# Encoder block on one core: the second MLP product as seven block products instead of eight, with weight sums made in DRAM

## What is computed

```
u = _rms(h, norm_mlp)
h = h + square(relu(u @ w_mlp_in)) @ w_mlp_out      # w_mlp_in 1024 x 4096, w_mlp_out 4096 x 1024
return _rms(h, norm_final)[:, N_META:]
```

## Time and profile before

| | |
|---|---|
| Median of three runs | 1323.64 us (1323.58 to 1324.17) |
| Profiled execution, its own time | 1323.88 us |
| Its span, first to last instruction | 1322.1 us |
| TensorE clock granted, mean over the span | 0.993 of full |
| Busy share of the span: PE, DVE, ACT, POOL | 97%, 49%, 35%, 32% |
| Matmuls of the second MLP product | 1152 |
| DMA over the span | 96.17 MB, mean 73 GB/s |

### The profile page before, as it was taken

The page is one execution under the profiler, slowest core; times in us unless marked ns, Lnnn a source line. Parts: engine busy times, 40 slices in busy tenths (PEclk is TensorE's granted clock), DMA queues, the critical chain, the costliest instruction groups (busy, mean ns, idle before and its releaser), DMA issues.

```text
span 1322.1 us, 18548 instructions
## 1 busy us (share of the span) xinstructions
PE 1283.5 (97%) x7181; PEld 1111.3 (84%) x7181; DVE 651.1 (49%) x743; ACT 461.1 (35%) x681; POOL 428.7 (32%) x244
## 2 busy tenths in 40 slices
PE   5999999999999999989999999999999999999996
PEld 4888888888889898878888888888888888888885
DVE  4116999999977777783732131111111233343334
ACT  5234211222266675643521341222222322233335
POOL 1453222233342333327322222222222222222234
PEclk8999999999999999999999999999999999999998
DMA  5222222333211011033352212222222121111112
GB/s 181 73 64 65 64 63 64 100 108 108 87 45 29 20 33 43 21 91 105 102 202 91 64 48 63 61 60 62 60 63 62 64 79 64 64 64 64 64 48 96
DMA packets 123907, 96.17 MB, mean 73 GB/s; under 512 B 9695, under 2 KB 106013, under 8 KB 123852
## 3 DMA queue, kind: packets, MB, share of 16 engines
q1 hardware_dynamic: 121548, 89.12, 22.5%
q10 hardware_dynamic: 2304, 6.29, 1.2%
HBM read 85.96 MB, written 9.44 MB: 72 GB/s over the span
## 4 chain that ended last, share of the span: by engine, by line
PE 86%; issue 4%; DVE 3%; ACT 3%; POOL 2%; DMA 1%; SPq 0%; ACTq 0%; POOLq 0%; DVEq 0%
PE psum L317 54%; PE psum L1671 23%; PE psum L1547 3%; PE psum L1577 2%; POOL wlo L304 1%; PE psum L1512 1%; PE psum L1435 1%; PE psum L1559 1%; DMA xt<-in_x_prompt 1%; ACT junk L823 1%; DVE ptlo L1038 1%; DVE olo L1103 1%; DVE negmax L1026 0%; PE psum L1678 0%; ACT uhi L506 0%
## 5 line engine op out<-in xcount | busy, mean ns | idle before, releaser
L304 POOL TENSOR_TENSOR wlo<-raw,whi 128x1024 fp32r<-128x1024 f32 (+2 forms) x144 | 335.3, 2329 | 724.4 <-ACT whi L299 724.2
L299 ACT ACTIVATE whi<-raw 128x1024 fp32r<-128x1024 f32 (+2 forms) x144 | 146.7, 1018 | 293.4 <-PE psum L1671 207.1
L946 DVE SCALAR_TENSOR_TENSOR psum<-cs,convw,psum 128x799 f32<-128x799 f32 x196 | 189.4, 1048 | 0.0
L1229 DVE TENSOR_TENSOR hidlo<-hid,hidhi 128x1536 fp32r<-128x1536 f32 x32 | 82.2, 2569 | 169.7 <-ACT hidhi L801 169.7
L317 PE MATMUL psum<-uhi,whi 128*128 128x512 f32 x592 | 152.3, 338 | 0.8 <-POOL wlo L304 0.8
L317 PE MATMUL psum<-uhi,wlo 128*128 128x512 f32 x592 | 152.9, 339 | 0.0
L317 PE MATMUL psum<-ulo,whi 128*128 128x512 f32 x592 | 152.6, 339 | 0.0
L1671 PE MATMUL psum<-whi,hidhi 128*128 128x512 f32 x384 | 149.4, 389 | 0.0
L1671 PE MATMUL psum<-whi,hidlo 128*128 128x512 f32 x384 | 149.4, 389 | 0.0
L1671 PE MATMUL psum<-wlo,hidhi 128*128 128x512 f32 x384 | 149.4, 389 | 0.0
L1239 DVE SCALAR_TENSOR_TENSOR hid<-psum,rbc 128x768 f32 (+1 forms) x32 | 30.6, 958 | 216.6 <-PE psum L317 216.6
(11 more groups left out here) (227 smaller groups left out, 2079.3 us busy)
## 6 DMA issues: line engine op xcount, KB each, us to landing
raw<-in_w_in SPq DMA_DIRECT2D x38, 512.0 KB, 4.1
raw<-in_w_mlp_in SPq DMA_DIRECT2D x32, 512.0 KB, 4.0
raw<-in_w_mlp_out SPq DMA_DIRECT2D x32, 512.0 KB, 3.5
gates<-gout ACTq DMA_DIRECT2D x16, 384.0 KB, 2.3
gin<-gates SPq DMA_DIRECT2D x16, 384.0 KB, 3.1
raw<-in_w_o_attn SPq DMA_DIRECT2D x8, 512.0 KB, 3.8
raw<-in_w_conv_out SPq DMA_DIRECT2D x8, 512.0 KB, 3.9
raw<-in_w_out SPq DMA_DIRECT2D x8, 512.0 KB, 3.4
```

The lines of the kernel that those rows point to most:

```text
L299: nc.scalar.activation(whi[:, c % 2, 0:w], raw[:, c % 4, 0:w], ACT.Copy).then_inc(hi_ready, 1)
L304: gp.tensor_tensor(out=wlo[:, c % 2, 0:w], in0=raw[:, c % 4, 0:w], in1=whi[:, c % 2, 0:w].bitcast(F32), op=ALU.subtract).then_inc(lo_ready, 1)
L946: ins = nc.vector.scalar_tensor_tensor(out=out, in0=src, scalar=w, in1=a, op0=ALU.mult, op1=ALU.add)
L1229: nc.vector.tensor_tensor(out=hidlo[c % 2][:, :, :], in0=hid[:, ds(i * 8 + 2 * c, 2), :], in1=hidhi[c % 2][:, :, :].bitcast(F32), op=ALU.s ...
```

## The change

The two operands of the second product are cut into 2x2 blocks: tokens in halves of 384 by alternate 256-row groups of the contraction, and those groups by columns in halves of 512. Seven products of block sums replace the eight block products. Each runs over 8 steps of 256 rows and 3 tiles of 128 tokens, so a unit is 18 matmuls of 128x128 by 128x512, and there are 56 units, 1008 matmuls. Results are added to or subtracted from `h1` by DVE, 36 additions of 128x512 in place of 12.

- Of the seven weight blocks four are sums of two. They are made in DRAM, in `wsums`, during the first MLP product: SP issues a copy of one summand with each unit's load, and POOL, behind `wlo` of the next unit, issues an accumulating DMA of the other. 32 copies and 32 accumulating DMAs, 512 KB each.
- A fifth (product 3, units 24 to 31) is a difference. It is made in SBUF: the block is loaded to `raw`, negated in place by ACT two units ahead, and POOL issues an accumulating DMA of the other block onto it: 8 of each.
- In five of the seven products the hidden operand is a difference of two blocks, made by DVE (`hmix`, 128x768).
- DVE makes the low part of the weights in place of POOL. High and low parts are rings of three instead of two.
- A step of DVE: low weights of m, `hmix` of m+1, `hidlo` of m, then one `y_add` of the product before (6 in the first 6 of 8 units, or 3). The banks of one product are added while the next one runs, which uses three others.
- Squares, means and outputs of the first 384 tokens move into products 5 and 6; after the last matmul three tiles are left instead of six. `yout` is gone; the output is made in `h1`.

The PE, ACT, DVE, POOL and SP programs of this part are written out over `for m in range(56)`. The diff, cut to its core:

```diff
+SUMS = (((0, 0), (1, 0)), ((1, 0), (1, 1)), ((0, 1), (1, 1)), ((0, 0), (0, 1)))
+MIX = (
+    dict(a=((1, 1),), b=((0, 0), (1, 0)), to=((0, 0, 1), (1, 0, 1))),
+    dict(a=((0, 0), (0, 1)), b=((1, 1),), to=((0, 0, 1), (0, 1, -1))),
+    dict(a=((0, 1), (1, 1)), b=((1, 0), (1, 1)), to=((0, 0, 1),)),
+    dict(a=((0, 0), (1, 1)), b=((1, 1), (0, 0)), to=((0, 0, 1), (1, 1, 1)), negate=True),
+    dict(a=((0, 0),), b=((0, 1), (1, 1)), to=((0, 1, 1), (1, 1, 1))),
+    dict(a=((1, 0), (1, 1)), b=((0, 0),), to=((1, 0, 1), (1, 1, -1))),
+    dict(a=((1, 0), (0, 0)), b=((0, 0), (0, 1)), to=((1, 1, 1),)),
+)
+Y_LEFT, Y_RIGHT, Y_SCALE = 5 * STEPS, 6 * STEPS - 3, 6 * STEPS + 2
...
 # SP
+            def sum_copy(c, jj):
+                wait_apart(sp, copy_landed[c], jj * 16)
+                sp.dma_start(sum_place(c, jj), sum_part(c, jj, 0)).then_inc(copy_landed[c], 16)
...
                     columns(wi, U_IN, i, c, ds(i * (4 * P) + c * P, P))
+                    sum_copy(c, i)
+            for m in range(FF_UNITS):
+                if m < 4:
+                    sp.wait_ge(lo_ready, U_FF + m - 3)
+                else:
+                    sp.wait_ge(wmlo_ready, m - 3)
+                if m % STEPS == 0 and mix_of(m)[0]["b"] in SUMS:
+                    sp.wait_ge(sums_landed[SUMS.index(mix_of(m)[0]["b"])], 16 * STEPS)
+                sp.dma_start(raw_block(m), wm_block(m, 0)).then_inc(raw_landed[m % 4], 16)
...
 # ACT
+            def mix_negate(m):
+                if m < FF_UNITS and mix_of(m)[0].get("negate", False):
+                    act.wait_ge(raw_landed[m % 4], (U_FF // 4 + m // 4 + 1) * 16)
+                    nc.scalar.activation(raw[:, m % 4], raw[:, m % 4], ACT.Copy, scale=-1.0).then_inc(wneg_ready, 1)
+            def mix_hi(m):
+                if mix_of(m)[0].get("negate", False):
+                    act.wait_ge(wsum_landed[m % 4], summed_before(m + 1, m % 4) * 16)
+                else:
+                    act.wait_ge(raw_landed[m % 4], (U_FF // 4 + m // 4 + 1) * 16)
+                act.wait_ge(unit_used, U_FF + m - 2 if m > 2 else U_FF - 1 + m if m < 2 else U_FF)
+                nc.scalar.activation(whf[m % 3], raw[:, m % 4], ACT.Copy).then_inc(wmhi_ready, 1)
+                if m == 0:
+                    act.wait_ge(u2_half_used, 1)
+                    act.wait_ge(hid_ready, 4)
+                elif len(mix_of(m)[0]["a"]) > 1:
+                    act.wait_ge(hmix_ready, mixed_before(m + 1))
+                nc.scalar.activation(hidhi[m % 3][:, :, :], hid_source(m), ACT.Copy).then_inc(hidhi_ready, 1)
...
+            for m in range(1, FF_UNITS):
+                mix_negate(m + 2)
+                mix_hi(m)
...
 # DVE
+            def mix_lo(m):
+                dve.wait_ge(wmhi_ready, m + 1)
+                nc.vector.tensor_tensor(out=wlf[m % 3], in0=raw[:, m % 4], in1=whf[m % 3].bitcast(F32),
+                                        op=ALU.subtract).then_inc(wmlo_ready, 1)
+                mix_hidden(m + 1)
+                dve.wait_ge(hidhi_ready, m + 1)
+                nc.vector.tensor_tensor(out=hidlo[m % 3][:, :, :], in0=hid_source(m), in1=hidhi[m % 3][:, :, :].bitcast(F32),
+                                        op=ALU.subtract).then_inc(hidlo_ready, 1)
...
+            for m in range(1, FF_UNITS):
+                mix_lo(m)
+                p, n = m // STEPS - 1, m % STEPS - 1
+                if p >= 0 and 0 <= n < TT * len(MIX[p]["to"]):
+                    if n == 0:
+                        dve.wait_ge(unit_used, U_FF + (p + 1) * STEPS)
+                    y_add(p, n)
+                if m == Y_SCALE:
+                    y_mean(0)
+                    dve.wait_ge(gfinal_landed, 16)
+                if Y_SCALE < m <= Y_SCALE + TT:
+                    y_finish(m - Y_SCALE - 1)
...
 # POOL
+            def sum_add(c, jj):
+                gp.wait_ge(copy_landed[c], jj * 16 + 16)
+                gp.dma_start(sum_place(c, jj), sum_part(c, jj, 1), accum_op=ALU.add).then_inc(sums_landed[c], 16)
...
+                    if not (isinstance(i, int) and i == KF // 4 - 1 and c == 3):
+                        lo_unit(gp, U_IN, i, c + 1)
+                    sum_add(c, i)
...
+                if mix.get("negate", False):
+                    gp.wait_ge(wneg_ready, negated_before(m + 1))
+                    gp.dma_start(raw_block(m), wm_block(m, 1), accum_op=ALU.add).then_inc(wsum_landed[m % 4], 16)
...
 # PE
+            for m in range(FF_UNITS):
+                p, jj = m // STEPS, m % STEPS
+                pe.wait_ge(wmlo_ready, m + 1)
+                pe.wait_ge(hidlo_ready, m + 1)
...
+                if p > 1 and jj == 0:
+                    pe.wait_ge(y_ready, posted(p - 1))
...
```

More of the change, by code:

```diff
@@ L76, with mix_of, mixed_before, summed_before @@
 U_FF = U_IN + KF
-U_END = U_FF + KF
+STEPS = 8
+U_END = U_FF + 7 * STEPS
+SUMS = (((0, 0), (1, 0)), ((1, 0), (1, 1)), ((0, 1), (1, 1)), ((0, 0), (0, 1)))
[8 more added lines that the diff above has]
+)
+MIXES = len(MIX)
+FF_UNITS = MIXES * STEPS
+THIRD = 384
+TT = THIRD // P
+FF_BANKS = ((4, 5, 6), (0, 1, 2))
+def mix_of(m):
+    return MIX[m // STEPS], m % STEPS
+def mixed_before(m):
+    return sum(len(mix_of(x)[0]["a"]) > 1 for x in range(m))
+def summed_before(m, c):
+    return sum(mix_of(x)[0].get("negate", False) for x in range(c, m, 4))
+def negated_before(m):
+    return sum(mix_of(x)[0].get("negate", False) for x in range(m))
+def posted(p):
+    return sum(TT * len(x["to"]) for x in MIX[:p])
+Y_FINAL = [[max(posted(p) + TT * n + i % TT + 1 for p, x in enumerate(MIX) for n, (a, b, _) in enumerate(x["to"])
+                if (a, b) == (i // TT, half)) for i in range(NT)] for half in range(2)]
+Y_LEFT, Y_RIGHT, Y_SCALE = 5 * STEPS, 6 * STEPS - 3, 6 * STEPS + 2
+def y_squares(half, i):
+    return [(0, 0), (0, 1), (0, 2), (1, 0), (1, 1), (1, 2), (0, 3), (0, 4), (0, 5), (1, 3), (1, 4), (1, 5)].index((half, i))
 VEC = {}
@@ L350, in sum_squares, with wm_block, sum_part, sum_place @@
             mm.then_inc(ss_mm, 1)
+        wm = t["w_mlp_out"][0].rearrange("(u a b p) n -> p u a b n", a=2, b=2, p=P)
+        def wm_block(m, which):
+            mix, jj = mix_of(m)
+            if len(mix["b"]) > 1 and not mix.get("negate", False):
+                return wsums[SUMS.index(mix["b"]), jj]
+            b, half = mix["b"][which]
+            return wm[:, jj, :, b, half * HALF:(half + 1) * HALF]
+        def sum_part(c, jj, which):
+            b, half = SUMS[c][which]
+            return wm[:, ds(jj, 1), :, b, half * HALF:(half + 1) * HALF].rearrange("p u a n -> p (u a) n")
+        def sum_place(c, jj):
+            return wsums[c, ds(jj, 1)].rearrange("u p a n -> p (u a) n")
+        def raw_block(m):
+            return raw[:, m % 4].rearrange("p (a n) -> p a n", a=2)
+        def hid_block(m, which):
+            mix, jj = mix_of(m)
+            half, b = mix["a"][which]
+            return hid_pairs[:, jj, :, b, half * THIRD:(half + 1) * THIRD]
+        def hid_source(m):
+            return hmix[m % 2][:, :, :] if len(mix_of(m)[0]["a"]) > 1 else hid_block(m, 0)
         block = ctx.enter_context(nc.Block())
@@ L806, in in_step @@
                     start = isinstance(i, int) and i == 0
-                    if not start:
+                    if isinstance(i, int) and i == KF // 4 - 1 and c == 3:
+                        mix_hi(0)
+                    elif not start:
                         hi_unit(act, U_IN, i, c + 1)
@@ L819, in y_square @@
             def y_square(half, i):
-                n = NT * half + i
-                act.wait_ge(y_ready, n + 1)
-                wait(act, y_sq, n)
+                act.wait_ge(y_ready, Y_FINAL[half][i])
+                wait(act, y_sq, y_squares(half, i))
                 nc.scalar.activation(junk2[:, :], h1[:, i, half * HALF:(half + 1) * HALF], ACT.Square,
                                      accum_out=halfsq[:, half, i:i + 1]).then_inc(y_sq, 1)
[L826 to L839, removed]
@@ L840, in _, with y_rms @@
[L840 to L850 removed]
+            def y_rms(i):
+                act.wait_ge(y_ms, i // TT + 1)
+                act.wait_ge(y_sq, y_squares(1, i) + 1)
                 nc.scalar.activation(root[:, i:i + 1], halfsq[:, 1, i:i + 1], ACT.Sqrt, bias=meansq[:, i:i + 1],
@@ L858, in _ @@
+            for i in range(TT, NT):
+                y_square(0, i)
+            for i in range(TT, NT):
+                y_square(1, i)
+                y_rms(i)
+                y_scale_left(i)
         @block.vector
@@ L1235, in in_step @@
                     if isinstance(i, int) and i == KF // 4 - 1 and c == 3:
-                        hid_lo(0, 0, 0)
+                        mix_lo(0)
                     dve.wait_ge(unit_used, i * 4 + (U_IN + c + 1))
```

164 lines of the change are left out of this document (84 added, 80 removed).

## The result

The changed kernel takes 1290.8 us in the median (1289.4 to 1291.6 in four runs) against 1323.7: a ratio of 0.9748, 95% interval 0.9735 to 0.9762. The forecast was 1290.5. The profiled execution has a span of 1289.1 us, 33.0 less than the span before.

What follows compares the result with a forecast made beforehand. TensorE was taken to bound both MLP products, a chain of small operations the end. Span 1322.1 - 32.6 - 3.4 + 1.6 + 1.0 = 1288.7, plus 1.8 around it: 1290.5 us; range 1286 to 1313.

Steps and rivals of the forecast that it cites:

- What bounds it: Both MLP products are bound by TensorE, with 0.2267 us from matmul to matmul; the end by a chain of small operations.
- TensorE, 32.6 us: Second product: 1008 matmuls in place of 1152 at 0.2267 us each save 32.6 us.
- DVE: Second product: a full step of DVE takes 3.82 us, below the unit's 4.08, with 0.958 us per 128x768 operation.
- The boundary, +1.6: Start of second product: unit 1 can't be prepared under the first product, so PE waits for it, +1.6 us.
- Products 5 and 6, +1.0: Added squares, means and outputs make three DVE steps 4.7 us for 4.08 and use up the slack: +1.0 us.
- Product 3, nothing: Sums in SBUF, at 7 us each, give units of 4.15 us for 4.08; 8 x 0.07 us is within the slack.
- which the slack takes: Product 3: if sums halve the DMA rate, the extra 8 x 0.42 = 3.4 us fits the 3.6 us of slack.
- The rule of two source reads: A reducing DMA reads two sources at half a plain one's rate: 3.0 us of DMA engines per sum in product 3.
- The end, 3.4: After the last matmul three tiles are left instead of six: 7.2 us instead of 10.6, a gain of 3.4.
- Sums in DRAM: Under the first product, a copy and a sum with each unit's load take 6.3 of 8.33 us: hidden, no cost.
- L taken as 7: Time for one accumulating DMA of 512 KB to land, assumed 7 us: a load's time for each of two reads.
- The slower rival: Sums in DRAM exceed 8.33 us each, queue up and stop PE at the boundary; 1367 us at 11 us each; chance 0.11.

Runs made afterwards that it cites:

- the run without gaps: Changed kernel with unit 1 prepared early and seven buffers for product 3's blocks: 1288.2 us, ratio 0.9732, against 1291.3 us beside it.
- the third set: Runs in which the changed kernel was measured a third time, with no edit, beside later variants: 1291.3 us, ratio 0.9751 to the kernel before.

## Why the prediction was right

**What bounds it:** right. PE's starts stayed 0.227 apart, and the eight plain products showed that 30.9 of the 33 us are the matmuls' count.

**TensorE, 32.6 us:** right, within 0.1, as the run without gaps measures: 228.28 us for 260.92.

**DVE:** right, and for the reason given. Taking the 0.958 us of the earlier trace rows for 768 and not 1.28 rested, in this stage, on one row, the first `hidlo`; the run with POOL's `wlo` back makes that 2.2 to 2.7 us.

**The boundary, +1.6:** 1.36 and 0.08, by the chain that was written down. Relu and square end where they were put (1.17 and 2.05 us after the boundary); the weights then follow the square at once and not 0.26 us later as in the earlier trace rows, which is the difference.

**Products 5 and 6, +1.0:** wrong, nothing. Three steps of DVE in a row did run longer than a unit, but 4.33 us each and not 4.7. The prediction added durations here, where its own slack went by spacing (3.49 for a full step, not 3.82). With 4.33 the three cost 0.75 us, and the slack was enough.

**Product 3, nothing:** wrong by 0.7 us in the profiled execution, 0.2 and 1.05 in the two others of the same kernel. The step that failed is "which the slack takes", and with it the sign "no wait of ACT for the sums in product 3". ACT waits for the load ahead of each negation (12.7 us in eight waits), which the prediction had no term for, and for the sum at units 30 and 31 (3.3 us in two waits). The demand was put a little low: 47.9% of the 56 us from 1128 to 1184 are 26.8 us of the DMA engines for eight sums, 3.3 each and not 3.0, beside a load of 1.5. But demand alone does not make the gap. The run without sums in DRAM has the same share in product 3, 0.91, and the same waits, and loses nothing there; the one with unit 1 early loses 2.6 us in gaps. What decides between them is open.

The rule of two source reads that was weighed there, of the Trainium skill's page "Collectives: The Full Stack" (Part 3), is borne out against a load: 3.0 us of the DMA engines for 1.5 to 1.8. Against a plain copy in DRAM, 1.1 to 1.2, a sum takes over 2.5 times as much. One reading is off: the earlier trace rows have a share of 0.17 in the second product, not 18%. The load of 1.5 us stands all the same, since some of the 32 loads are issued ahead of that window.

**The end, 3.4:** 3.2.

**Sums in DRAM:** L taken as 7, measured 7.4 and 7.3; POOL's issue is bounded by 0 and 2.4 and took 1.05 us (1.20 onto SBUF). Nothing was held up. The slower rival's mechanism exists, but the runs mend it in two points: what counts is the demand on the DMA engines, whose share twice the sums put above 1, and the first to be late is a load, not the sum.

So the gain of 33 us is forecast by the right mechanism, but the agreement of 1290.5 with 1290.8 is luck in its last microsecond. It holds two errors, +1.0 us in products 5 and 6 and -0.9 in product 3 (gaps of 0.7 and 0.2 for refilling), that cancel; the rest is 0.2 each at the boundary and the end, against each other, and the 0.4 us by which this execution was later before the first product.

## What to carry to other kernels

Price an engine that is to take over work with the durations that it has while no other engine holds it up: one row without overlap tells more than a mean of 32 with it. A transfer under a stage bound by TensorE was free here with a DMA share of up to 0.86 and was not at 1.08; then the load that the stage waits for is the one that comes late. Add up steps of an engine by the spacing of its starts, not by durations. When units get half as long, look at the first two after a change of stage: their preparation had a cover that is gone.

## What the runs showed of the hardware that I had not expected

An accumulating DMA of 512 KB takes 3.0 us of the 16 DMA engines in DRAM and 3.3 onto SBUF, a copy in DRAM 1.1 to 1.2, a load into SBUF 1.5 to 1.8. The copy is cheaper than the load, yet takes nearly twice as long to land in the same stage (7.2 for 4.1 us).

Of the spread from run to run (2 to 4 us) some 1.4 us is made in the first 50 us, before anything that was changed. The window from 36.8 to 48.6 us (transposes of the input) in the changed kernel's profile and in the third set's:

```profile
36.80:48.60 11.80, 11.80 (x71) 10.44 (x71) 2.97 (x5) 2.89 (x5) 3.57 (x4) 1.00 0.44 135
```

```profile
36.80:48.60 11.80, 11.80 (x62) 10.55 (x63) 2.15 (x5) 2.44 (x4) 3.58 (x4) 0.86 0.44 135
```

Ahead of it PE had pauses (7.3 to 7.6 us busy of 8.8). In one execution it then has the 2.4 GHz level throughout, in the other the 1.2 GHz level for part of it, and 60 matmuls take 11.5 us for 10.1. Of these 1.4 us 1.0 is left when the first MLP product begins (781.38 for 780.36). So a gain of 1 us is better read between the first and the last matmul of the stage than in the total.
